# Index queries, index keys and sparse keys turned by VectorE and placed by GpSimd, with the index scores of two pairs in one group

## What is computed

```python
bk = _rope(_rmsnorm(b_k.reshape(bsz, seq, 1, B_HEAD_DIM), b_k_norm), b_rot)[:, :, 0]
iq = _rope(i_q.reshape(bsz, seq, IDX_HEADS, IDX_DIM), i_rot)
ik = _rope(_rmsnorm(i_k, idx_k_norm)[:, :, None, :], i_rot)[:, :, 0]
iw = i_w * (IDX_HEADS ** -0.5 * IDX_DIM ** -0.5)
...
rel = jax.nn.relu(jnp.einsum('bqhd,bkd->bqhk', qib, k_idx).astype(jnp.float32))
score = jnp.einsum('bqh,bqhk->bqk', wb.astype(jnp.float32), rel)
score = jnp.where(mask, score, -jnp.inf)
_, sel = lax.top_k(score, top_k)
```

## Time and profile before

| | us |
|---|---|
| timed runs, median of 3 | 2885.08 (2885.07 to 2885.09) |
| the profiled execution, its own time | 2884.71 |
| its span in the trace | 2882.9 |
| TensorE busy (matmuls) | 2875.4 |
| VectorE busy | 1823.1 |
| ScalarE busy | 1339.0 |
| GpSimd busy | 648.2 |

### The profile page before, as it was taken

The page is one execution under the profiler, slowest core; times in us unless marked ns, Lnnn a source line. Parts: engine busy times, 40 slices in busy tenths (PEclk is TensorE's granted clock), DMA queues, the critical chain, the costliest instruction groups (busy, mean ns, idle before and its releaser), DMA issues.

```text
span 2882.9 us, 35147 instructions
## 1 busy us (share of the span) xinstructions
PE 2875.4 (100%) x12964; PEld 2381.4 (83%) x12964; DVE 1823.1 (63%) x2223; ACT 1339.0 (46%) x1570; POOL 648.2 (22%) x1033
## 2 busy tenths in 40 slices
PE   9999999999999999999999999999999999999999
PEld 8888888888888888888888888888888888888887
DVE  7589866687655555545575898656775555555554
ACT  5445554554444444444444455455544444344443
POOL 0025224144122312300000242231441213213000
PEclk9999999999999999999999999999999999999999
DMA  7666666775666666666666666666766666666665
GB/s 247 183 185 195 202 186 189 232 235 190 192 192 194 194 190 195 193 194 192 193 193 176 196 190 197 191 189 228 238 191 194 191 194 192 193 193 194 193 194 170
DMA packets 291293, 567.35 MB, mean 197 GB/s; under 512 B 18985, under 2 KB 24945, under 8 KB 291185
## 3 DMA queue, kind: packets, MB, share of 16 engines
q1 hardware_dynamic: 283888, 540.54, 61.9%
q10 hardware_dynamic: 7296, 25.44, 2.7%
HBM read 551.23 MB, written 14.68 MB: 196 GB/s over the span
## 4 chain that ended last, share of the span: by engine, by line
PE 94%; POOL 2%; DVE 2%; issue 1%; ACT 0%; DMA 0%; ACTq 0%; SPq 0%; DVEq 0%
PE acc L456 61%; PE acc L461 30%; POOL small L387 2%; PE acc L503 1%; DVE w_lo L1197 1%; PE acc L501 1%; DVE nat L1197 0%; DVE small L1197 0%; ACT w_hi L807 0%; PE acc L514 0%; PE acc L494 0%; PE acc L509 0%; DVE small L1215 0%; DMA w_raw<-in_w_in_dram 0%; PE acc L515 0%
## 5 line engine op out<-in xcount | busy, mean ns | idle before, releaser
L1197 DVE TENSOR_TENSOR w_lo<-w_raw,w_hi 128x1024 fp32r<-128x1024 f32 x1024 | 1259.9, 1234 | 1013.4 <-ACT w_hi L807 1008.8
L807 ACT ACTIVATE w_hi<-w_raw 128x1024 fp32r<-128x1024 f32 x1024 | 1084.5, 1060 | 1480.1 <-PE acc L461 1447.6
L456 PE MATMUL acc<-w_hi,opa_hi 128*128 128x512 f32 (+1 forms) x2364 | 930.7, 394 | 0.6 <-ACT w_hi L807 0.6
L456 PE MATMUL acc<-w_hi,opa_lo 128*128 128x512 f32 (+1 forms) x2364 | 918.0, 388 | 0.0
L456 PE MATMUL acc<-w_hi,opb_hi 128*128 128x512 f32 x1728 | 672.9, 389 | 0.1
L456 PE MATMUL acc<-w_hi,opb_lo 128*128 128x512 f32 x1728 | 672.3, 389 | 0.0
L461 PE MATMUL acc<-w_lo,opa_hi 128*128 128x512 f32 (+1 forms) x2364 | 629.3, 388 | 0.0
L456 PEld LDWEIGHTS acc<-w_hi,opa_hi 128*128 128x128 f32 x2364 | 444.0, 188 | 93.8 <-issue 6.4
L461 PEld LDWEIGHTS acc<-w_lo,opa_hi 128*128 128x128 f32 x2364 | 443.1, 188 | 90.9 <-DVE w_lo L1197 0.4
L456 PEld LDWEIGHTS acc<-w_hi,opa_lo 128*128 128x128 f32 x2364 | 444.1, 188 | 87.6
L461 PE MATMUL acc<-w_lo,opb_hi 128*128 128x512 f32 x1728 | 461.8, 389 | 0.0
(11 more groups left out here) (188 smaller groups left out, 1136.3 us busy)
## 6 DMA issues: line engine op xcount, KB each, us to landing
w_raw<-in_w_gate_up_dram SPq DMA_DIRECT2D x352, 512.0 KB, 4.4
w_raw<-in_w_in_dram SPq DMA_DIRECT2D x336, 512.0 KB, 3.7
w_raw<-in_w_down_dram SPq DMA_DIRECT2D x176, 512.0 KB, 4.4
w_raw<-in_w_branch_dram SPq DMA_DIRECT2D x64, 512.0 KB, 4.6
w_raw<-in_w_out_dram SPq DMA_DIRECT2D x64, 512.0 KB, 4.3
gate_store<-nat ACTq DMA_DIRECT2D x24, 512.0 KB, 3.8
arena<-gate_store ACTq DMA_DIRECT2D x24, 512.0 KB, 5.5
w_raw<-in_w_kv_b_dram SPq DMA_DIRECT2D x16, 512.0 KB, 4.3
```

Source lines behind the costliest of these rows:

```text
L456: pe.matmul(bank(pair, t, width), op[j][:, kt + k, t * P:(t + 1) * P], w_hi[:, s, k, 0:width], start=(first and k == 0 and j == 0), stop=F ...
L807: return act.activation(out, in_, ACT.Copy, scale=scale)
L1197: return dve.tensor_tensor(out, a, b, op)
```

## The change

The index queries, the index keys and the sparse keys are no longer transposed by TensorE and copied by ScalarE. VectorE turns them in 32x32 blocks behind step 1 of block 0 (`turn_index`: one transpose of 128x1024 and two of 128x256), and GpSimd places them: 16 copies for the queries, 32 of 32x64 for the keys. All four pairs of queries then stand in the place that the a keys take later (`iq_t` is `ak_t`), so the a keys' placement waits for the last index scores. VectorE's turning of the a queries waits for `i_placed`, as it writes the buffer that the index queries were placed from.

The scores of blocks 0 and 1 go. Blocks 2 and 3 compute two pairs each, in one group behind step 2 (`two_pairs`), into banks 6 and 7 and banks 4 and 5. The relus stand behind steps 3 and 5 and the sums ahead of steps 4 and 6. ScalarE's `ckv_split` moves from step 5 to step 4.

```diff
+        iq_t, ik_t = ak_t, part(1536, SEQ)
+        k_turned = part(3072, 2 * SEQ).rearrange("p (q k t s) -> p q k t s", q=4, k=2, t=NT)
...
             for l in range(DEPTH):
+                pool.wait_ge(i_rows, l + 1)
+                place(iq_t, pre_turned)
+                for k, cols in enumerate((ik_t, bk_t[:, :])):
+                    k_dst = cols.rearrange("p (t i s) -> p t i s", t=NT, i=4)
+                    for q in range(4):
+                        for i in range(4):
+                            ins = pool.tensor_copy(k_dst[32 * q:32 * q + 32, :, i], k_turned[32 * i:32 * i + 32, q, k])
+                ins.then_inc(i_placed, 1)
                 pool.wait_ge(aq_rows, l + 1)
...
                 pool.wait_ge(ak_rows, l + 1)
+                pool.wait_ge(i_scored, (l + 1) * PROJ2)
                 place(ak_t, ak_turned).then_inc(a_placed, 1)
...
-                        def pair_t():
-                            if h + e == l * PROJ2:
-                                pe.wait_ge(i_staged, l + 1)
-                                for t in range(NT):
-                                    pe.transpose(acc[:, 4, SEQ + t * P:SEQ + (t + 1) * P], ik_rows[:, t], ident[:, :])
-                                    pe.transpose(acc[:, 5, t * P:(t + 1) * P], proj[:, t, BK:BK + P], ident[:, :])
-                            at = IQ + (i * 2 + e) * P
-                            for t in range(NT):
-                                mm = pe.transpose(acc[:, 4, t * P:(t + 1) * P], proj[:, t, at:at + P], ident[:, :])
-                            mm.then_inc(i_t, 1)
...
-                        whole(n, e * UB, opa, e, {4: pair_t, 5: pair_scores},
+                        def two_pairs():
+                            if e == 0:
+                                pe.wait_ge(i_placed, l + 1)
+                            else:
+                                pe.wait_ge(i_relu, l * PROJ2 + 2)
+                            for pair in (2 * e, 2 * e + 1):
+                                for m in range(2):
+                                    r = slice(64 * m, 64 * m + 64)
+                                    scores(acc[:, 6 - 2 * (pair % 2) + m, 0:KEYS], [iq_t[r, pair]], [ik_t[r, :]],
+                                           i_scored if m else None)
+
+                        whole(n, e * UB, opa, e, {2: two_pairs} if i else {},
...
-                        through(n, nq, e * UB, {4: pair_sb, 6: pair_relu, 7: leave} |
-                                ({5: ckv_split} if i * 2 + e == PROJ2 - 1 else {}))
+                        through(n, nq, e * UB, {7: leave} |
+                                ({3: lambda n: pair_relu(2 * e), 5: lambda n: pair_relu(2 * e + 1)} if i else {}) |
+                                ({4: ckv_split} if i * 2 + e == PROJ2 - 1 else {}))
...
+                    def turn_index():
+                        turn(pre_turned, proj[:, :, IQ:IK])
+                        for k, rows in enumerate((ik_rows, proj[:, :, BK:BV])):
+                            ins = dve.transpose(k_turned[:, :, k].rearrange("p q t s -> p t q s"),
+                                                rows.rearrange("p t (q s) -> p t q s", s=32))
+                        ins.then_inc(i_rows, 1)
+
+                    def turn_aq():
+                        wait(i_placed, l + 1)
+                        turn(pre_turned, proj[:, :, AQ:AK]).then_inc(aq_rows, 1)
...
-                    before, after = {7: [pair_sums]}, {2: [norm_a], 3: [norm_b]}
+                    before, after = {}, {2: [norm_a], 3: [norm_b]}
+                    if i >= 2:
+                        before = {4: [lambda: pair_sums(2 * i - 4)], 6: [lambda: pair_sums(2 * i - 3)]}
                     if i == 0:
 
-                        after[0] = [index_rows, norm_bk, lambda: dve.sem_inc(i_staged, 1), index_weights]
+                        after[0] = [index_rows, norm_bk, index_weights]
+                        after[1] = [turn_index]
...
                     if i == 1:
-                        after[4] = [lambda: turn(pre_turned, proj[:, :, AQ:AK]).then_inc(aq_rows, 1)]
+                        after[4] = [turn_aq]
```

More of the change, by code:

```diff
@@ L197, in hybrid_trunk @@
         qk_n = part(0, 512)
-        iq_t, ik_t = part(1024, SEQ), part(1536, SEQ)
         bq_t = proj[:, :, BQ:BQ + 2 * SEQ]
@@ L244, in hybrid_trunk @@
         ao_rows, ao_t, ao_hi, ao_lo = sem("ao_rows"), sem("ao_t"), sem("ao_hi"), sem("ao_lo")
-        i_staged, i_t, i_sb, i_scored, i_relu, i_summed = (sem("i_staged"), sem("i_t"), sem("i_sb"),
-                                                           sem("i_scored"), sem("i_relu"), sem("i_summed"))
+        i_rows, i_placed, i_scored, i_relu, i_summed = (sem("i_rows"), sem("i_placed"), sem("i_scored"),
+                                                        sem("i_relu"), sem("i_summed"))
         lam_dots, lam_exp = sem("lam_dots"), sem("lam_exp")
@@ L587, in _ @@
                     g = l * ACT_GROUPS + PROJ1 + i * 2
-                    h = l * PROJ2 + i * 2
                     for e in range(2):
                         pe.wait_ge(act_emptied, g + (e + 1))
-                        def pair_t():
-                            if h + e == l * PROJ2:
-                                pe.wait_ge(i_staged, l + 1)
-                                for t in range(NT):
-                                    pe.transpose(acc[:, 4, SEQ + t * P:SEQ + (t + 1) * P], ik_rows[:, t], ident[:, :])
-                                    pe.transpose(acc[:, 5, t * P:(t + 1) * P], proj[:, t, BK:BK + P], ident[:, :])
-                            at = IQ + (i * 2 + e) * P
-                            for t in range(NT):
-                                mm = pe.transpose(acc[:, 4, t * P:(t + 1) * P], proj[:, t, at:at + P], ident[:, :])
-                            mm.then_inc(i_t, 1)
[L602 to L607, removed]
-                        whole(n, e * UB, opa, e, {4: pair_t, 5: pair_scores},
+                        def two_pairs():
[9 more added lines that the diff above has]
+                        whole(n, e * UB, opa, e, {2: two_pairs} if i else {},
                               N if i or e else STUB)
@@ L917, in _, with pair_relu @@
                     n, nq = bases(l, PROJ1 + i * 2)
-                    h = l * PROJ2 + i * 2
                     for e in range(2):
[L920 to L930, removed]
+                        def pair_relu(pair):
+                            act.wait_ge(i_scored, l * PROJ2 + pair + 1)
+                            act.wait_ge(i_summed, l * PROJ2 + pair + 1)
+                            b = 6 - 2 * (pair % 2)
+                            act.activation(s_sb, acc[:, b:b + 2, 0:KEYS], ACT.Relu).then_inc(i_relu, 1)
                         def leave(n):
@@ L1496, in norm_b, with pair_sums @@
                         normed(b1, 1, B_DIM, r_bq[:, :, ds(i, 1)], gain(GBQ, B_DIM, 1), ROT["b"], ROPE_AT["b"])
-                    def pair_sums():
-                        wait(i_relu, l * PROJ2 + i + 1)
+                    def pair_sums(pair):
+                        wait(i_relu, l * PROJ2 + pair + 1)
                         for m in range(2):
@@ L1502, in pair_sums @@
                                 ins = dve.scalar_tensor_tensor(score_i[:, a:b], s_sb[:, m, a:b],
-                                                               iws[:, t, ds(i * 2 + m, 1)], score_i[:, a:b],
+                                                               iws[:, t, ds(pair * 2 + m, 1)], score_i[:, a:b],
                                                                ALU.mult, ALU.add)
@@ L1507, in pair_sums @@
                         ins.then_inc(i_summed, 1)
-                        wait(i_summed, l * PROJ2 + i + 2)
+                        wait(i_summed, l * PROJ2 + pair + 2)
+                    def turn_index():
[7 more added lines that the diff above has]
+                        turn(pre_turned, proj[:, :, AQ:AK]).then_inc(aq_rows, 1)
                     def turn_ckv():
```

## The result

The changed kernel takes **2891.59 us** (median; 2890.35 to 2893.15), the kernel before 2885.07 beside it: 6.5 us more. The ratio is 1.0023, with a 95% interval of 1.0015 to 1.0030. The forecast was 2890.4 in a range of 2886.5 to 2895.

A forecast was written before the change was run, and what follows sets the result against it. TensorE bounds the kernel, with VectorE equally binding in the stub block. That block's +2.8 less 0.17 gave 2.6 us a layer, 5.3 for two, on 2885.08: 2890.4 us, range 2886.5 to 2895.

The forecast's parts named there:

- The bound: TensorE is busy 2875.4 of 2882.9 us; in the stub block (392 columns wide) VectorE is as much the bound.
- lo 8: Low parts (w_lo) for unit 0 of the block behind the stub block: ready at 165.7, block end 2.8 us later.
- What TensorE is spared: Transposes gone (1.83) and four score groups made two (0.44): 2.27 us a layer if nothing waited, 2.10 in stub block.
- Contention: GpSimd's copies slow VectorE's two normalisations and two w_lo in the stub block by 1.6 us.
- The w_lo at 221.04: VectorE instruction in the earlier profile, at its plain length; cited as evidence that GpSimd's copies do not hold VectorE.
- no contention: Rival: GpSimd's copies do not hold VectorE; stub block ends 1.2 later, 2887.2 us; chance 0.18 with little contention.
- the 5 us worked out from half of 0.7: Alternative VectorE delay per layer: some 15 two-input instructions each held half a copy of about 0.7 us; not adopted.
- 0.17: Us per layer that blocks 1 to 3 together give back: block 1 gains 1.37, blocks 2 and 3 lose 0.60 each.
- i_placed: VectorE's block 1 wait for GpSimd's placement: little forecast; as rival it reaches TensorE, 2898.4 us at 0.73 a copy, chance 0.12.
- The rival's price of 3.2 us for each further 0.1: Cost per layer once a 32x64 GpSimd copy exceeds 0.61 us and VectorE's wait reaches TensorE; rival's chance 0.12.
- the 187.8 of the text: Time until which VectorE's block 1 wait costs nothing: block 2 unit 1's w_lo is wanted at 190.2, turn and w_lo take 2.4.
- Chances: Forecast as told 0.55, no or little contention 0.18, i_placed 0.12, faster 0.07, rest 0.08; slower 0.37, same 0.56, faster 0.07.

The follow-up runs named there:

- neither: Changed kernel without VectorE's three stub-block transposes and GpSimd's 48 copies, constant fills instead; 2884.54 us, 0.6 under the kernel before.
- before_turns: Kernel before the change, with only the three VectorE transposes added behind step 1 of the stub block, result unused; 2887.69 us, 2.5 over.
- late: Changed kernel with sparse-key norm, turning, index weights and scores later, keys placed first, queries in their own buffer; 2882.91 us, 2.3 under the kernel before.
- no_copies: Changed kernel with GpSimd's 48 copies left out, three constant fills instead, VectorE's transposes kept; 2886.87 us, 1.7 over the kernel before.
- own_buffer: Changed kernel with index queries turned into their own buffer, so the a queries' turning does not wait for GpSimd; 2891.41 us, 6.2 over the kernel before.
- filler: Changed kernel with eight unused 128x128 matmuls on TensorE behind step 6 of each layer's stub block; 2890.18 us, 5.0 over the kernel before.

## Why the prediction was right, point by point

- **The bound.** TensorE was spared its 24 transposes and lost more in waits for VectorE, in the stub block and at lo 8 alone: the reading of the earlier trace rows. `neither`, `before_turns` and `late` bear it out from three sides.
- **What TensorE is spared.** 2.27 a layer was forecast; with no wait `late` gains 2.43. The term that was a little off is the merged group: 1.87 in place of 1.97.
- **The transposes** took 1.81 for 1.9.
- **Contention.** 1.6 was forecast. The normalisations grew by 0.66 and 0.76 (0.68 and 0.53 forecast), w_lo of unit 7 by 0.1; `no_copies` puts the effect on TensorE at 1.7. Two readings of rows beside it were wrong, without harm to the sum. The w_lo at 221.04, named in favour of no contention, ran when GpSimd had stopped (its copies end at 209.16 + 11.71 = 220.87). And 0.7 us is the mean distance of the 32x256 copies, their own holds included; one alone took 0.39, so the 5 us worked out from half of 0.7 was too high by that alone.
- **Lo 8** was forecast 2.8 late. Without the clock it is 1.57 + 1.17 = 2.74 late in own_buffer (its stub block and its first unit of block 1), and blocks 1 to 3 gave back 0.17, as forecast: 2.57 a layer, 5.14 in all against 5.3. That this 0.17 came out to the digit is luck: with no waits the three blocks gain 0.33 (`late`), and the restart behind lo 8, which the prediction has not, takes 0.16 of it.
- **i_placed.** VectorE's wait was forecast at nearly nothing and was 2.85: the 16 query copies took 13.3, not 11.7, as six of them and not four stood beside a large w_lo. The copies of 32x64 took (184.9 - 170.2) / 32 = 0.46 (0.45 forecast), and this agreement is luck in part: both figures are means over copies held up by VectorE and copies that were not. Where VectorE did not wait and ran on, they took 0.52 (`own_buffer`) and 0.58 (`late`). The rival's price of 3.2 us for each further 0.1 leaves out that a waiting VectorE lets the copies run at 0.27 each. TensorE felt none of it, as the 187.8 of the text allows.
- **What was missing.** The measured 6.5 is 1.4 above these 5.1. The clock's fall is 0.4 to 0.9 of it in the two traces, and the merge block 0.1 and 1.2. How the 1.4 of the timed runs is shared between the two is not shown: `filler`, which keeps the clock up, was measured at 5.0, but the runs of the changed kernel with the clock up were no faster than the others. The range had room for both, though neither was named as a term of it.
- **Chances.** 0.37 was on slower by over 0.2%, and 0.56 on no change that can be told. The measured ratio, 1.0023, is just beyond that bound, and its interval (1.0015 to 1.0030) holds the bound too. Without the 1.4 us above the ratio would have been 1.0018, on the other side of the bound.

## What to carry to other kernels

Work taken off the busiest engine is worth only as much as the engine that serves it has in hand at that place: read, unit by unit, when each operand is ready and when it is used, and add what the change puts there. The next hand-over has a reserve of its own: of the 4.9 us that `late` wins, 1.4 were lost again where the probabilities were ready only 1.9 us ahead of need. Work that moves to GpSimd also has a price on VectorE, which holds while both run; place it where VectorE has time in hand. With the same turning and placing put behind the tight stretch, a loss of 6.5 us became a gain of 3.4.

## What the runs showed of the hardware that I had not expected

TensorE's clock fell from 2.4 to 1.2 GHz behind waits of 0.58, 0.52 and 1.88 us inside an else busy stream, in some executions and layers and not in others; with the last of them filled by matmuls, or at 1.1 us, its mean stayed at 1.000 in every run. A fall cost 0.35 to 0.53 us, since part of it hid in the next wait.

A GpSimd copy and a VectorE instruction with two inputs held each other up, one at a time. Alone, a copy of 32x64 took 0.23 us and one of 32x128 0.29; beside a 128x1024 w_lo both sizes took 1.1 to 1.3. A transpose, with its one input, held none. This copy of `late` ran inside VectorE's 128x1024 transpose of 165.52 to 166.77:

```profile
165.91 0.23 POOL L406 COPY small<-small 32x64 f32<-32x64 f32 x1
```

So the price of a row of small copies is set less by their size than by what VectorE runs beside them: 16 of 32x128 in 7.17 us are 0.45 each, with two held up, and 32 of half that size were 0.46 each.
